# Pairing the row pairs of the second window pair as (0,1) ... (8,9) and 10, in an encoder layer on one core

## The reference

```
h2 = _rms(x, norm2_g)
g = jax.nn.silu(_dwconv(h2 @ ffn_w_gate, ffn_dw_w, ffn_dw_b))
x = x + (g * (h2 @ ffn_w_up)) @ ffn_w_down
```

## Time and profile before

| | |
|---|---|
| Median of 3 runs | 2567.1 us (2565.86 to 2567.85) |
| Profiled execution | 2563.86 us, span 2561.8 us |
| Busy in the span | TensorE 98%, weight loads 88%, VectorE 76%, ScalarE 56%, GpSimd 12% |
| Mean granted TensorE clock | 0.995 of 2.4 GHz |
| First part | up to about 1488 us |
| Window pair 0 | about 1488 to 2023 us |
| Window pair 1 | about 2023 to 2561.8 us |

### The profile page before, as it was taken

How to read it: one execution, slowest core, us unless ns; L and a number is a source line. 1 busy time by engine, 2 the same in 40 slices (tenths; PEclk the granted TensorE clock), 3 DMA queues, 4 the chain that set the end, 5 groups by cost and what they waited for, 6 DMA issues and landing times. The chain is left out here.

```text
span 2561.8 us, 36076 instructions
## 1 busy us (share of the span) xinstructions
PE 2519.3 (98%) x12663; PEld 2242.3 (88%) x12663; DVE 1936.6 (76%) x3228; ACT 1431.1 (56%) x2578; POOL 319.8 (12%) x483
## 2 busy tenths in 40 slices
PE   8999999999999999999999999999999899999997
PEld 7877777788878888888888899999999899999997
DVE  5886767887878697969794678687687887867864
ACT  6345544468436852784474356665655665655654
POOL 1110121201011102110101101100100111011011
PEclk9999999999999999999999999999999999999999
DMA  9988988834464456445537736735746675475465
GB/s 361 387 315 313 339 329 347 305 113 169 175 236 144 148 217 244 154 152 217 203 132 295 261 98 154 174 106 132 171 108 182 145 160 127 113 170 133 111 151 108
DMA packets 166834, 505.80 MB, mean 197 GB/s; under 512 B 28832, under 2 KB 37536, under 8 KB 147200
## 3 DMA queue, kind: packets, MB, share of 16 engines
q1 hardware_dynamic: 119344, 336.60, 37.6%
q0 software_dynamic: 47312, 166.91, 24.4%
HBM read 350.07 MB, written 153.36 MB: 197 GB/s over the span
## 5 line engine op out<-in xcount | busy, mean ns | idle before, releaser
L2037 DVE TENSOR_TENSOR part_lo<-part_raw,part_hi 128x512 fp32r<-128x512 f32 x462 | 316.7, 689 | 237.1 <-ACT part_hi L1561 234.3
L2357 PE MATMUL bank<-hw_hi,weights 128*128 128x462 f32 (+3 forms) x1408 | 420.7, 373 | 0.0
L1858 DVE SCALAR_TENSOR_TENSOR cc<-win,par,cc 128x512 f32<-128x512 f32 x600 | 408.3, 744 | 0.0
L1561 ACT ACTIVATE part_hi<-part_raw 128x512 fp32r<-128x512 f32 x462 | 285.7, 628 | 176.2 <-DMA part_raw<-w_pass_t 71.1
L2308 PE MATMUL bank<-h_hi,weights 128*128 128x512 f32 x1104 | 355.6, 395 | 0.0
L2521 PE MATMUL bank<-mid,part_hi 128*128 128x414 f32 x1232 | 337.3, 354 | 13.7 <-DVE pair_y L2122 6.0
L2357 PEld LDWEIGHTS bank<-hw_hi,weights 128*128 128x128 f32 x1408 | 264.7, 188 | 37.3 <-issue 12.2
L2357 PE MATMUL bank<-hw_lo,weights 128*128 128x464 f32 (+3 forms) x704 | 259.2, 368 | 0.0
L2308 PEld LDWEIGHTS bank<-h_hi,weights 128*128 128x128 f32 x1104 | 207.9, 188 | 51.7 <-issue 6.1
L2521 PEld LDWEIGHTS bank<-mid,part_hi 128*128 128x128 f32 x1232 | 231.9, 189 | 20.5 <-DVE part_lo L2037 9.9
L2503 PE MATMUL bank<-T_hi,part_hi 128*128 128x414 f32 (+1 forms) x704 | 246.0, 349 | 2.1 <-DVE e L2061 2.1
(11 more groups left out here) (231 smaller groups left out, 4596.1 us busy)
## 6 DMA issues: line engine op xcount, KB each, us to landing
weights<-weight_scratch SPq DMA_DIRECT2D x88, 1024.0 KB, 7.3
y_pair_t<-pair_y POOLq DMA_DIRECT2D x140, 414.0 KB, 7.8
wraw<-w_ffn_t SPq DMA_DIRECT2D x88, 512.0 KB, 3.3
part_raw<-w_ffn_t SPq DMA_DIRECT2D x176, 256.0 KB, 2.8
weight_scratch<-weights POOLq DMA_DIRECT2D x22, 1024.0 KB, 8.0
wraw<-w_down_t SPq DMA_DIRECT2D x44, 512.0 KB, 3.3
part_raw<-down_sums SPq DMA_DIRECT2D x88, 256.0 KB, 4.5
part_raw<-w_pass_t SPq DMA_DIRECT2D x66, 256.0 KB, 5.9
```

The lines of the kernel that those rows point to most:

```text
L1561: nc.scalar.activation(p_hi[k % HI_RING][:], p_raw[part_of(k)][:], ACT.Copy).then_inc(s_whi, 1)
L1858: nc.vector.scalar_tensor_tensor(acc, win[i][:, tap:tap + TB], w_tap, acc, ALU.mult, ALU.add).then_inc(s_cv, 1)
L2037: nc.vector.tensor_tensor(p_lo[part_of(k)][:], p_raw[part_of(k)][:], p_hi[k % HI_RING][:].bitcast(F32), ALU.subtract).then_inc(s_wlo, 1)
L2357: mm = nc.tensor.matmul(out, l[:, k, :], r[:, k, cols], start=(k == 0 and j == 0), stop=(k == KT - 1 and j == 2))
```

## The change

In the second window pair the passes become [0,1], [2,3], [4,5], [6,7], [8,9], [10]: the pass of a single row pair is the last one. `PASSES` and `PASS_OF` are now kept per window pair. The order of the first window pair stays as it was, step for step. In the second, the first down product comes after step 4.6 (it was 2.6), and the list ends 21.6 21.2 21.3 21.7 21.4, then D5:5, 3, 2, 1, 6, 7, 4 of row 10 alone (before: 21.7, D5:5 row 9, 21.4, and then 13 more down steps of rows 9 and 10). In the last pass of both window pairs, the eviction of outputs 0 to 2 moves to the end of the list of the product's own last step, and output 3 stays at the head of the next list. Operand B12 of the next window gets another buffer (that of the rounded part of T2) and is loaded one product earlier. `COMBO_AT` becomes 13, 16, 19, 23, 26, 29, 33, 36, 39, 43, 46 (it was 12, 16, 20, ... 52).

The diff, cut to its core:

```diff
-COMBO_AT = [12 + 4 * r for r in range(FT // 2)]
+COMBO_AT = [13 + 10 * r // 3 for r in range(FT // 2)]
...
-PASSES = [[0]] + [[i, i + 1] for i in range(1, ROW_PAIRS, 2)]
-PASS_OF = {i: n for n, p in enumerate(PASSES) for i in p}
+PASSES = [[[0]] + [[i, i + 1] for i in range(1, ROW_PAIRS, 2)] for _ in range(PAIRS - 1)]
+PASSES.append([[i, i + 1] for i in range(0, ROW_PAIRS - 1, 2)] + [[ROW_PAIRS - 1]])
+PASS_COUNT = len(PASSES[0])
+PASS_OF = [{i: n for n, p in enumerate(of) for i in p} for of in PASSES]
...
-                if _behind and (_i > 1 or len(_behind[0]) > 1 or _p in (6, 3, 1, 4)) and not (_i % 2 and _s == 0 and _p in (1, 5, 4)):
+                _open = _open or _p == 6
+                if _behind and _open and (_i > 1 or len(_behind[0]) > 1 or _p in (6, 3, 1, 4)):
                     PROD += _behind.pop(0)
-    _behind = [("D", _q, len(PASSES) - 1, _p, _r) for _p in DOWN_ORDER for _r in PASSES[-1]]
-    PROD += _behind[:1] + [("P", _q, GROUPS - 1, 4)] + _behind[1:]
+    _behind = [("D", _q, PASS_COUNT - 1, _p, _r) for _p in DOWN_ORDER for _r in PASSES[_q][-1]]
+    _ahead = len(PASSES[_q][-1]) - 1
+    PROD += _behind[:_ahead] + [("P", _q, GROUPS - 1, 4)] + _behind[_ahead:]
...
-    if PROD[_k][4] == PASSES[PROD[_k][2]][-1]:
-        if adds_sum(*PROD[_k][2:4]):
-            DVE_AT[_k + 1].insert(0, ("y_sum", _k))
+    if PROD[_k][4] == PASSES[PROD[_k][1]][PROD[_k][2]][-1]:
+        _side, _op = (DVE_AT, "y_sum") if adds_sum(*PROD[_k][2:4]) else (ACT_AT, "y_copy")
+        if PROD[_k][2] == PASS_COUNT - 1:
+            _side[_k].append((_op, _k, 0, KH - 1))
+            _side[_k + 1].insert(0, (_op, _k, KH - 1, KH))
         else:
-            ACT_AT[_k + 1].insert(0, ("y_copy", _k))
+            _side[_k + 1].insert(0, (_op, _k, 0, KH))
...
-        for _b, _p in (("B11", 1), ("B21", 2), ("B22", 3), ("B12", 7)):
+        for _b, _p in (("B11", 1), ("B21", 2), ("B22", 3), ("B12", 6)):
...
-        b_raw["B12"] = b_raw["T3"]
+        b_raw["B12"] = run(hi_at["T2"], ("B12_raw", [P, KH, B_PITCH], F32))[0][:, :, 0:TQ]
...
-                    act.wait_ge(s2_t, 4 * q + int(b[1]))
+                    act.wait_ge(s2_t, 4 * q + max(int(b[1]), 3 * (b == "T2")))
...
-                if q > 0 and t != "T3":
-                    dve.wait_ge(s_used, SLOTS + at(GROUPS * q - 1, {"T1": 5, "T2": 6, "T4": 4}[t]) + 1)
+                if q > 0:
+                    dve.wait_ge(s_used, SLOTS + at(GROUPS * q - 1, {"T1": 5, "T2": 6, "T3": 7, "T4": 4}[t]) + 1)
```

More of the change, by code:

```diff
@@ L380 @@
 for _q in range(PAIRS):
-    _behind = []
+    _behind, _open = [], False
     for _i in range(ROW_PAIRS):
-        if _i > 0 and PASS_OF[_i] != PASS_OF[_i - 1]:
-            _behind = [[("D", _q, PASS_OF[_i - 1], _p, _r) for _r in PASSES[PASS_OF[_i - 1]]] for _p in DOWN_ORDER]
+        if _i > 0 and PASS_OF[_q][_i] != PASS_OF[_q][_i - 1]:
+            _F = PASS_OF[_q][_i - 1]
+            _behind, _open = [[("D", _q, _F, _p, _r) for _r in PASSES[_q][_F]] for _p in DOWN_ORDER], False
         for _s in range(2):
@@ L409, in down_phase @@
 def down_phase(q, F, p):
-    return len(DOWN_ORDER) * (len(PASSES) * q + F) + DOWN_ORDER.index(p)
+    return len(DOWN_ORDER) * (PASS_COUNT * q + F) + DOWN_ORDER.index(p)
 def adds_sum(F, p):
-    return p == 1 or (p == 6 and F == len(PASSES) - 1)
+    return p == 1 or (p == 6 and F == PASS_COUNT - 1)
 def holds(F, p):
-    return p == 2 or (p == 3 and F == len(PASSES) - 1)
+    return p == 2 or (p == 3 and F == PASS_COUNT - 1)
 EVICTED, Y_TILE, Y_TILES = {}, {}, []
 for _q in range(PAIRS):
-    for _F in range(len(PASSES)):
+    for _F in range(PASS_COUNT):
         for _p in DOWN_ORDER:
@@ L454, in mid_reader @@
         if mid_seat(j) == mid_seat(i):
-            return AT_PROD["D", q, PASS_OF[j], p, j]
+            return AT_PROD["D", q, PASS_OF[q][j], p, j]
     return None
@@ L1017, in load_pair_window @@
                 else:
-                    sp.wait_ge(s_used, SLOTS + at(GROUPS * q - 1, {"B11": 1, "B21": 2, "B22": 3, "B12": 7}[b]) + 1)
+                    sp.wait_ge(s_used, SLOTS + at(GROUPS * q - 1, {"B11": 1, "B21": 2, "B22": 3, "B12": 6}[b]) + 1)
                 sp.dma_start(b_raw[b][:], h2_d.rearrange("k p n -> p k n")[:, half:half + KH,
@@ L1596, in pair_tap0, with pair_y_copy @@
                     if u % ROW_PAIRS == 0:
-                        act.wait_ge(s_ys, KH * (EVICTED[u // ROW_PAIRS - 1, len(PASSES) - 1, 6] + 1))
+                        act.wait_ge(s_ys, KH * (EVICTED[u // ROW_PAIRS - 1, PASS_COUNT - 1, 6] + 1))
                 nc.scalar.activation(v_buf[x][:], src[:, 0:TP], ACT.Copy,
                                      scale=col("ffn_w", FFN_TAPS * hidden_tile(gi, x))).then_inc(s_c1, 1)
-            def pair_y_copy(k):
+            def pair_y_copy(k, first, last):
                 q, F, p = PROD[k][1:4]
-                for o, tile in y_outputs(k):
+                for o, tile in y_outputs(k)[first:last]:
                     phase_done(act, k, o)
-                    if p == 3 and F == len(PASSES) - 1:
+                    if p == 3 and F == PASS_COUNT - 1:
                         act.wait_ge(s_mlo, H_PLAIN + 7 * ROW_PAIRS * (q + 1))
@@ L1742, in _ @@
                     elif t[0] == "y_copy":
[L1743 removed]
+                        pair_y_copy(*t[1:])
                     elif t[0] == "window_high":
@@ L2111, in pair_mid_low, with pair_y_sum @@
                                         mid2[:, seat_, B_ORDER.index(b), 0].bitcast(F32), ALU.subtract).then_inc(s_mlo, 1)
-            def pair_y_sum(k):
+            def pair_y_sum(k, first, last):
                 q, F, p = PROD[k][1:4]
                 before = EVICTED[q, F, 2 if p == 1 else 3]
-                for o, tile in y_outputs(k):
+                for o, tile in y_outputs(k)[first:last]:
                     phase_done(dve, k, o)
@@ L2251, in _ @@
                     elif t[0] == "y_sum":
-                        pair_y_sum(t[1])
+                        pair_y_sum(*t[1:])
                     elif t[0] == "low":
@@ L2511, in pair_down @@
                 a, b = p_hi[k % HI_RING], p_lo[part_of(k)]
-                first, last = i == PASSES[F][0], i == PASSES[F][-1]
+                first, last = i == PASSES[q][F][0], i == PASSES[q][F][-1]
                 for o in range(KH):
```

## The result

| | before | after |
|---|---|---|
| Median of 4 runs, us | 2566.48 (2564.93 to 2567.85) | 2594.41 (2590.53 to 2595.17) |
| Profiled execution: time, span | 2563.86, 2561.8 | 2590.53, 2588.4 |
| First product of window pair 0 starts | 1488.15 | 1502.79 |

The ratio is 1.0106 [1.0088, 1.0123]: 1.1% slower. The forecast was 2568.4 us (2563 to 2574), no difference. The spans differ by 26.6 us. Stage by stage: +14.6 in the first part; +2.3 among the products of window pair 0, where three idles of 0.4 to 1 us for `pair_y` stand that come and go from execution to execution of both kernels; +3.6 between the window pairs (from the start of 21.4 of window pair 0 to the first matmul of window pair 1); +6.1 behind 21.7 in the tail. Busy times are within 5 us of those of before: nothing was added, TensorE waits more and is busy 4.2 us longer, as more of its work falls on a low clock.

A forecast was written before the change was run, and what follows sets the result against it. TensorE, busy 98% of the span, was taken as the bound, with only three places mattering: -3.8 + 1.0 + 4.1 = +1.3 us on 2567.1 gives 2568.4 us, no difference, range 2563 to 2574 us.

The forecast's parts named there:

- Part 1: Combo slots in the first part: earlier last sums close a TensorE gap and its low clock, -3.8 us (-4.7 to +1.8).
- qk idle: TensorE's 2.08 us gap at about 377 us, waiting for VectorE's qk; claimed to close, with 1.7 us of low clock.
- Part 2: Between the window pairs: VectorE's list is the bound, the 5.63 us gap is split, not removed; +1.0 us (0 to +3.4).
- Part 3: The tail after the last passes: waits for T1 and for output tiles outweigh the shorter pass; +4.1 us (+1.0 to +8.4).
- t + 7.1: Tail: start of D5:5, 7.1 us after the end of step 21.7 (t), held by VectorE's T1 remainder; TensorE idle 3.1 us.
- the ring of four tiles: Tail: four output tiles, two per product; copies of D5:7 and D5:4 wait until adds of D5:1 and D5:6 land, 7.5 us.
- 2L - 9.8: Tail cost in us for a landing time L of both adds: +1.0 at 5.4, +8.4 at 9.1.
- Rival 1: Tail: adds crowd each other, copies of D5:7 and D5:4 wait for tiles; total +5.6, 2572.7 us; chance 0.2.
- Rival 2: First part: ending combo work also relieves the load before 411.63 and closes the 0.90 gap; -5.8, 2561.3 us; chance 0.1.
- Rival 3: Tail: no output tile is ever waited for, needing landings under about 3 us; in all -5.2, 2561.9 us; chance 0.03.
- signs named for a right forecast: No gap at 377; two gaps between pairs; tail idles of about 1.5 and 3 us, copies waiting for a pair_y DMA.
- signs for a wrong one: TensorE running D5:7 and D5:4 back to back, no gap between the pairs, or new gaps before 350 us behind input loads.

The follow-up runs named there:

- group 2: Kernel before with varied combo loads: new slots, store from constant 1.0020; slots 8 + 4r 1.0032; load behind input loads 1.0036 (new), 0.9984 (old); sums and store earlier 1.0022.
- group 1: Changed kernel with old combo slots 1.0041, also without eviction split 1.0030; kernel before with only the new slots 1.0065, with only the split 1.0013.
- group 3: Changed kernel with old combo slots: six more output tiles 1.0042; instead T1's and B22's remainders one list step earlier 1.0022.

## Why the prediction was wrong

**Part 1** failed: -3.8 us with ends of -4.7 and +1.8, measured +14.6. The step was "the existing waits cost TensorE one gap of 0.90, so I bound the new ones by two such gaps". It counted idles and did not work out how long SyncE would stand. Both numbers for that were at hand. The store is listed four slots behind its load, and seven of ten next loads now stand three slots behind, so those waits grow by up to a slot each: 34.8 us became 85.8. And the 11.02 us for `xs` showed that an input load behind such a wait had no slack left: the idle behind it grew from 0.90 to 4.67 us, and a new one of 5.83 us came behind the `xt` loads, each with a low clock behind it. The gain claimed was not read rightly either. The 3.4 us by which `qk` was to start earlier left out that VectorE waits there for the keys (group 2). The qk idle fell by 1.0 us, not 2.1, with the new slots, and was 2.87 us when the last sums only moved to slot 51; that no low clock followed in the changed kernel is as foretold.

**Part 2**: +1.0 (ends 0 and +3.4), measured +3.6 between the two executions compared, and 2.5 between the medians of group 1. The piece that was worked out, the sums that wait for their banks, measured 1.1 us where 0.7 was foretold. The premise that failed is that VectorE's list runs on without a pause and that "all behind it is the same work": it paused 1.74 and 0.51 us for ScalarE. The first pause comes from the split together with the new B12 buffer. The prediction says of B12 only that its earlier load is "worth nothing, since VectorE never waited for it"; that its new buffer makes T2's rounded part wait for the sum T3 was put at nothing. The low clock at the last steps, an end of 1.7 us in the prediction, shows only in the second pause, as VectorE's last remainder set the start of the last step.

**Part 3**: +4.1 (ends +1.0 and +8.4), measured +6.1. D5:5 was to start at t + 7.1 and started at 2554.75 - 2547.5 = t + 7.2; its low clock cost 5.25 x 0.33 = 1.7 as said; D5:6 was summed at t + 22.5 (22.3 foretold). From there it was late: GpSimd issued D5:6's second add 0.7 us later than assumed, it landed in 8.3 us instead of 7.5, and the last one in 6.8 instead of 6.3. That is the 2.0 us. But "here the ring of four tiles bites" is only half of it: without the ring the end is no earlier (group 3). The price 2L - 9.8 has no meaning of its own; L is what the spacing of the adds makes of it. The unchanged tail varies by 4 us from execution to execution, so it is in part luck that the sum came within 2.0 us.

**The rivals.** Rival 1 foretold the tail's crowding rightly, but not its size (+8.4), and the slowdown came mostly from elsewhere. Rival 2 did happen in part, the low clock behind the cat load went, and was outweighed. Rival 3, landings of about 3 us, did not: with ten adds close together the median landing was 6.8. Of the signs named for a right forecast, those in the tail came (idles of 1.58 and 3.17 us, copies of D5:7 and D5:4 waiting for a DMA of `pair_y`). Of the signs for a wrong one, "new gaps before 350 us behind input loads" is the one that came. The opening statement that the largest single wait is the 5.6 us for VectorE's sums overlooked the 7.6 us for the first weights, which changes nothing in the sum. The chance of slower, 0.21, was too low, as it came from the tail alone: part 1 had no bad end worth the name.

## What to carry to other kernels

Where a load waits in an in-order queue for a store of its own buffer, count in slots: the load's distance to the next load against its distance to the store. If the first is smaller, the wait grows by up to a slot per load, and everything queued behind it, however unrelated, loses that slack. Before crediting an operation with the wait behind it, look at what it stood behind itself. A buffer that is shared in a new way adds a wait for the engine that writes it, also when the one that reads it never waited. Work that ends a chain in bulk transfers, as here, is timed by issue of the first and drain of the rest, not by the buffers between. And one execution against one other tells little about a stage that varies by 2 to 8 us.

## What the runs showed of the hardware

Adds of 414 KB that accumulate in HBM followed each other at 2.6 us each when close together, whether four or ten tiles fed them, at a DMA share of 1.08 and 0.97. A single one took 6.8 us to land at the median of ten in the changed kernel, and 10.6 us at the median of the six that did not wait for a tile of the ring.

After an idle of 5.83 us the granted clock was 0.55 for 4.8 us, and it was 0.50 for 5.0 us after idles of 2.27, 3.07 and 1.60 us between 2024.9 and 2034.6. After an idle of 1.77 us it was 1.00, where after one of 1.90 us in the kernel before it had been 0.60.

One and the same load (`kw`, 128x640) took 8.1, 10.5 and 12.5 us to land in three kernels that differ in the slots of the combo loads.
